# A decoder layer on one core: a new mixing order from engine queues, rotations in one scratch slot, gates that may move, and an output projection finished token tile by token tile

## The reference, cut to what matters

```python
h = rms_norm(x, ln_mix_pre);  p = h @ w_in                    # split into the branches' inputs and 3 * 1024 gate logits
y_a = dsa_attention(rotate(q), rotate(k), v, rotate(iq), rotate(ik), iw)   # index scores, top 128 keys of a query, softmax
y_b = rms_norm(gated_delta_rule(conv_silu(q, k, v), g, beta)) * silu(z)    # chunks, triangular inverse, scan
y_c = rms_norm(retention(rotate(q), rotate(k), v)) * silu(g)
merged = sum_i sigmoid(gate_i) * (y_i @ w_branch_i)
x = x + rms_norm(merged @ w_out, ln_mix_post)
x = x + rms_norm(square(relu(rms_norm(x, ln_mlp_pre) @ w_up)) @ w_down, ln_mlp_post)
```

## Time and profile before

| | |
|---|---|
| median of 3 runs | 2124.4 us (2123.76 to 2124.95) |
| the profiled execution | 2125.75 us, of which its span 2123.5 us |
| mean granted clock of TensorE | 0.961 of full |
| PE busy | 1977.4 us, 93% of the span |
| DVE, ACT, POOL busy | 47%, 21%, 53% |

### The profile page before, as it was taken

One profiled execution on the slowest core, in us unless ns is written; L12 is line 12 of the kernel. 1 busy time (PEld: TensorE's weight loads), 2 busy tenths in 40 slices (PEclk: granted clock), 3 DMA queues, 4 the chain that ended last, 5 costly groups with the idle time before them and its releaser, 6 DMA issues. The chain is left out here.

```text
span 2123.5 us, 25297 instructions
## 1 busy us (share of the span) xinstructions
PE 1977.4 (93%) x8942; PEld 1588.6 (75%) x8942; DVE 1004.9 (47%) x1616; ACT 450.9 (21%) x865; POOL 1130.0 (53%) x913
## 2 busy tenths in 40 slices
PE   7989978999998999999789899889999979999996
PEld 5856666778886888888668666667788868888885
DVE  4753666643434650361446436586334446404504
ACT  2152223321312100010112422242222131000101
POOL 4643331346665566666646424303567746666665
PEclk9999998999999999999889999899999989999998
DMA  6331220112322233222233212111224223223222
GB/s 251 100 110 58 57 81 24 57 60 99 139 97 82 80 99 99 96 92 99 96 133 99 95 60 72 60 40 50 70 96 143 90 69 100 98 92 98 99 98 79
DMA packets 73334, 192.07 MB, mean 90 GB/s; under 512 B 18528, under 2 KB 31008, under 8 KB 72224
## 3 DMA queue, kind: packets, MB, share of 16 engines
q1 hardware_dynamic: 46368, 173.22, 24.2%
q10 hardware_dynamic: 26880, 17.67, 2.8%
HBM read 179.81 MB, written 11.06 MB: 90 GB/s over the span
## 5 line engine op out<-in xcount | busy, mean ns | idle before, releaser
L803 POOL TENSOR_TENSOR w_lo<-raw,w_hi 128x1024 fp32r<-128x1024 f32 x296 | 726.5, 2455 | 24.7
L799 POOL TENSOR_TENSOR w_hi<-raw,tabs 128x1 fp32r<-128x1 f32 x296 | 65.5, 221 | 938.9 <-PE psD L838 724.5
L836 PE MATMUL psD<-a_hi,w_hi 128*128 128x512 f32 (+1 forms) x960 | 389.3, 406 | 15.5 <-DVE a_lo L1537 14.2
L837 PE MATMUL psD<-a_lo,w_hi 128*128 128x512 f32 (+1 forms) x960 | 378.5, 394 | 0.0
L838 PE MATMUL psD<-a_hi,w_lo 128*128 128x512 f32 (+1 forms) x960 | 378.4, 394 | 0.0
L800 POOL TENSOR_SCALAR w_hi<-raw 128x1023 fp32r<-128x1023 f32 x296 | 319.5, 1079 | 0.0
L836 PEld LDWEIGHTS psD<-a_hi,w_hi 128*128 128x128 f32 (+1 forms) x960 | 182.0, 190 | 60.1 <-DVE a_lo L1537 16.3
L837 PEld LDWEIGHTS psD<-a_lo,w_hi 128*128 128x128 f32 (+1 forms) x960 | 181.6, 189 | 41.4 <-issue 4.6
L838 PEld LDWEIGHTS psD<-a_hi,w_lo 128*128 128x128 f32 (+1 forms) x960 | 181.1, 189 | 41.9 <-issue 2.2
L836 PE MATMUL psM<-a_hi,w_hi 128*128 128x512 f32 x512 | 200.2, 391 | 0.3
L837 PE MATMUL psM<-a_lo,w_hi 128*128 128x512 f32 x512 | 199.3, 389 | 0.0
(11 more groups left out here) (238 smaller groups left out, 3091.4 us busy)
## 6 DMA issues: line engine op xcount, KB each, us to landing
raw<-in_ws SPq DMA_DIRECT2D x298, 512.0 KB, 3.3
out<-x SPq DMA_DIRECT2D x12, 512.0 KB, 2.6
tabs<-in_tab SPq DMA_DIRECT2D x2, 3072.0 KB, 12.9
x<-rows_d ACTq DMA_DIRECT2D x4, 1024.0 KB, 5.8
x<-out ACTq DMA_DIRECT2D x2, 2048.0 KB, 8.6
x<-in_x SPq DMA_DIRECT2D x4, 512.0 KB, 5.6
mt_d<-bw ACTq DMA_DIRECT2D x8, 256.0 KB, 2.3
x<-x_d ACTq DMA_DIRECT2D x8, 256.0 KB, 3.2
```

What stands on the lines that cost most here:

```text
L799: pool.tensor_tensor(w_hi[:, s, 0:1], raw[:, s, 0:1], T("ones")[:, 0:1], ALU.mult)
L803: pool.tensor_tensor(w_lo[:, s, :], raw[:, s, :], w_hi[:, s, :].bitcast(F32), ALU.subtract) \
L836: pe.matmul(out, lhi, rhi, start=start, stop=False)
L837: pe.matmul(out, lhi, rlo, start=False, stop=False)
```

## The change

The planner gets a clock for ACT, prices of four numbers (PE, ACT, DVE, and into how many pieces a step falls, so that engines overlap within it), widths for the attention steps, and 0.8 in place of 0.4 between steps of a stream. Scores with top-k and softmax with attention become two streams. The retention gates become a stream of their own, last in the list, which may run at any time (the last two only after the last rotation, whose scratch they overwrite). A rotation writes its cosine product straight to the destination and uses one scratch slot for the rest; the squares of `unit` and `fin` move to a new tile `sqs`.

Of the output projection two slabs stay in the stream. The other six are loaded by ACT's queue into memory that the branches have left, split by ACT and DVE in steps `stay` between the last merges, and stay there, so that PE can finish one token tile after the other (`out_tile`). The norm chain, the turning of x (`turn_x1`) and its split (`hi_x1`, `lo_x1`, 128 columns at a time) follow tile by tile; the first two slabs of the MLP run with 384 columns for tiles 0 to 2 and then with 128 columns for tile 3. The MLP's banks `psM` and `psD` change roles, `wide` is no longer zeroed (the first group copies into it), and the group loop is written out. In the diff the deepest indentation is reduced.

```diff
+STAYING = [("out", k, 2, half * S, S) for half, k in ((0, 4), (0, 6), (1, 0), (1, 2), (1, 4), (1, 6))]
+READY = ST - 1
...
-    slab = 2.6
-    cost = {"decay": (0, 1, .7), "prep": (2.7, 3.8, .7), "mt_out": (0, 0, .2), "blk_in": (0, 0, .2),
...
+    slab = 2.73
+    gate = (slab, .6, 0, 1)
+    cost = {"decay": (0, .6, 1.1, 1), "prep": (2.7, 1.2, 4.6, 2), "mt_out": (0, .1, 0, 1), "blk_in": (0, .1, 0, 1),
+            "solve": (0, 0, 7.5, 1), "y_out": (0, .2, 0, 1), "x_in": (0, .2, 0, 1), "lev": (0, 0, .9, 1),
+            "keys": (0, 0, 1.8, 1), "left": (.9, .6, 0, 1), "right": (1.8, 0, 1.8, 2), "scan_w": (.9, .6, 0, 1),
+            "scan_v": (1.8, .6, 0, 1), "scan_o": (2.7, .6, 1.6, 1), "ret": (4.3, .6, 2.4, 4), "turn": (0, 0, 1.6, 1),
+            "fin_sq": (0, .6, 0, 1), "fin": (.9, 1.2, 1.8, 1), "split": (0, .6, .9, 1), "half": (slab, 0, 0, 1),
+            "cv": (slab, .6, 0, 1), "rot": (slab, 1.2, .7, 1), "cg": (slab, .6, .7, 1), "z": (slab, .6, .7, 1),
+            "gate": gate, "mgate": gate, "mergeC": (slab, 0, 1.4, 1), "merge": (slab, 0, 3.2, 1)}
+    def takes(s):
+        w = s[1] + 1 if len(s) > 1 and s[0] in ("index", "top", "soft", "attend") else 0
+        if s[0] == "index":
+            return 1.75 * w, 8 * (.2 + .11 * w), 9 * (.13 + .17 * w), 8
+        if s[0] == "top":
+            return 0, 0, TOPK / TOPS / 4 * (.1 + .15 * w), 1
+        if s[0] == "soft":
+            return .86 * w, 4 * (.2 + .11 * w), 4 * (.6 + .32 * w), 4
+        if s[0] == "attend":
+            return 1.3 * w, .6 * w + .6, 0, w
+        return cost[s[0]]
...
-    attention = []
-    for tb in range(1, ST):
-        attention += [("index", tb)] + [("top", tb, part) for part in range(TOPS)]
-        for t in range(0 if tb == 1 else tb, tb + 1):
-            attention += [("soft", t), ("attend", t)]
-    attention += [("split", "C", h) for h in range(H)]
+    scores, softs = [], []
+    for tb in range(ST):
+        if tb:
+            scores += [("index", tb)] + [("top", tb, part) for part in range(TOPS)]
+        softs += [("soft", tb), ("attend", tb)]
+    softs += [("split", "C", h) for h in range(H)]
     dense = [("cv", i) for i in range(4)] + [("rot", r) for r in range(5, ROTS)] + [("cg", h) for h in range(H)]
-    dense += [("gate", "C", n) for n in range(KT)]
+    filler = [("gate", "C", n) for n in range(KT)]
...
-             ("soft", 0): [("turn", ROTS - 1)], ("gate", "C", 0): [("turn", ROTS - 1), ("fin", "C", 3)],
-             ("cg", 0): [("unit", 7)], ("split", "C", 0): [("fin", "C", 3)], ("mergeC", 0): [("split", "C", 3)],
+             ("soft", 0): [("turn", ROTS - 1)], ("gate", "C", 6): [("turn", ROTS - 1)],
+             ("cg", 0): [("unit", 7)], ("split", "C", 0): [("fin", "C", 3)], ("mergeC", 0): [("split", "C", 3), ("gate", "C", 7)],
              ("z", 0): [("split", "C", 3)], ("mgate", "A", 0): [("fin", "C", 3)],
              ("split", "A", 0): [("attend", ST - 1), ("mergeC", 3)]}
     for r in range(5, ROTS):
         after["turn", r] = [("rot", r)]
         after["rot", r] = [("turn", r - 2)]
-    shifts = 2.2
+    for tb in range(1, ST):
+        after["soft", tb] = [("top", tb, TOPS - 1)]
+        after["top", tb, TOPS - 1] = [("soft", tb - 1)]
...
-    dense = [s for d in dense for s in ([d] if d[0] == "split" else [("half", *d), d])]
+    dense, filler = ([s for d in what for s in ([d] if d[0] == "split" else [("half", *d), d])]
+                                     for what in (dense, filler))
     for s in list(after):
-        if s in dense:
+        if s in dense + filler:
             after["half", *s] = after.pop(s)
-    streams = [attention, rotations, chunks, even, odd + last, retention, dense]
+    streams = [scores, softs, rotations, chunks, even, odd + last, retention, dense, filler]
...
+    slabs = {len(streams) - 2, len(streams) - 1}
+    halved = None
     def ready(i):
+        if halved is not None and i in slabs and i != halved:
+            return 1e9
         return max([free[i]] + [ends.get(s, 1e9) for s in after.get(streams[i][0], ())])
...
+        if i in slabs:
+            halved = i if s[0] == "half" else None
+        t, c, d, k = takes(s)
+        begin = max(pe, at) if t else at
+        end = begin + t
         if t:
-            pe = max(pe, at) + t
+            pe = end
+        if c:
+            act = end = max(max(act, begin) + c, end + c / k + .2)
         if d:
-            dve = max(dve, at, pe + a if t or a else 0.0) + d
-        ends[s] = (dve if d else max(pe, at) + a) + (shifts if s[0] == "rot" else landing.get(s[0], 0))
-        free[i] = pe if streams[i] is dense else ends[s] + 0.4
+            dve = end = max(max(dve, begin) + d, end + d / k + .2)
+        ends[s] = end + landing.get(s[0], 0)
+        free[i] = pe if i in slabs else ends[s] + margin
...
-    o += [("split", "B", h) for h in range(H)] + merges("B", 0)
-    return o
+    tail = merges("B", 0)
+    for j in range(len(STAYING)):
+        tail.insert(5 + 2 * j, ("stay", j))
+    return o + [("split", "B", h) for h in range(H)] + tail
...
-    for half in range(2):
-        add(f"out{half}", *(("out", i, 2, half * S, S) for i in range(0, KT, 2)))
+    add("out0", *(("out", i, 2, 0, S) for i in range(0, STAYING[0][1], 2)))
...
+        with ExitStack() as o:
+            pg = sb("pg", [P, D], where=o)
+            s_hi = sb("s_hi", [P, len(STAYING), SLAB], F32R, where=o)
+            with ExitStack() as u:
+                s_raw = sb("s_raw", [P, len(STAYING), SLAB], where=u)
+            s_lo = sb("s_lo", [P, len(STAYING), SLAB], F32R, where=o)
...
+        def x1_T(t, k):
+            banks = (psM[0:2], psD[0:2], psM[0:2], psM[2:4])[t]
+            return banks[k // (KT // 2)][:, cut(k % (KT // 2))]
...
-        done(nslab([psM[t][:, :] for t in range(ST)], slab_in("out0", i), 2 * i, 2, S, i == 0, i == 3))
+        done(nslab([psM[t][:, :] for t in range(ST)], slab_in("out0", i), 2 * i, 2, S, i == 0, False))
     outs = [bank(DENSE["out1"] + t)[:, :] for t in range(ST)]
...
-    for i in range(3):
-        done(nslab(outs, slab_in("out1", i), 2 * i, 2, S, i == 0, False))
...
-    pe.wait_ge(sem("gained"), ST)
-    for t in range(ST - 1):
+    def out_tile(t):
+        for j, (_, k, ks, c, _) in enumerate(STAYING):
+            if t == 0:
+                pe.wait_ge(sem("s_lo"), j + 1)
+                pe.wait_ge(sem("a_lo"), KT + k + 2)
+            ins = nslab(outs if c else [psM[i][:, :] for i in range(ST)], j, k, ks, S,
+                        c > 0 and k == 0, k == KT - 2, ts=[t], w=(s_hi, s_lo))
+            if k == KT - 2:
+                ins.then_inc(sem("out_tile"), 1)
+    def turn_x1(t):
         pe.wait_ge(sem("diag_pre_mlp"), t + 1)
+        for i in range(2):
+            if t == 2:
+                pe.wait_ge(sem("a_lo"), 2 * KT + KT // 2 * (i + 1))
+            else:
+                pe.wait_ge(sem("gained"), (1, 2, None, 5)[t] + 2 * i)
+            for k in range(KT // 2 * i, KT // 2 * (i + 1)):
+                ins = pe.matmul(x1_T(t, k), x[:, t, cut(k)], wide[:, t, 0:P], start=True, stop=True)
+            ins.then_inc(sem("x1_turned"), 1)
+    for t in range(READY):
+        out_tile(t)
+    for t in range(READY - 1):
+        turn_x1(t)
+    out_tile(ST - 1)
+    turn_x1(READY - 1)
+    def up_tokens(i, t0, t1):
         for k in range(KT):
-            scaled_T(pe, (psM + psD)[k], t, k)
-    pe.wait_ge(sem("diag_pre_mlp"), ST)
-    for k in range(KT):
-        small_done(scaled_T(pe, (psM + psD)[k], ST - 1, k))
-    with pe.Fori(0, GROUPS) as g:
+            if i == 0:
+                pe.wait_ge(sem("a_lo"), 2 * KT + KT * (t1 - 1) + k + 1)
+            ins = tslab(psD[i][:, t0 * P:t1 * P], i % 2, ks=[k], cols=slice(t0 * P, t1 * P))
+        return ins
...
+            up_tokens(i, 0, READY)
+            if i == 1:
+                turn_x1(READY)
+                for j in range(2):
+                    done(up_tokens(j, READY, ST))
...
-            sig(act.copy(wt[to:to + n, r % 2, :], dbank(("rot", r))[at:at + n, :]),
+            sig(act.copy(wt[to:to + n, 6 + r % 2, :], dbank(("rot", r))[at:at + n, :]),
...
+    def stay(j):
+        if j == 0:
+            act.wait_ge(sem("stay_in"), 16 * len(STAYING))
+        sig(act.copy(s_hi[:, j, :], s_raw[:, j, :]), "s_hi")
...
+            act.wait_ge(sem("y_lo"), 3 * H)
+            for j in range(len(STAYING)):
+                act.dma_start(s_raw[:, j, :],
+                              wo[bass.ds(layer * len(STAYING) + j, 1)].rearrange("a p n -> (a p) n")) \
+                    .then_inc(sem("stay_in"), 16)
...
+    def hi_x1(t):
+        for k in range(KT):
+            act.wait_ge(sem("x1_turned"), 2 * t + k // (KT // 2) + 1)
+            sig(act.activation(a_hi[:, k, cut(t)], x1_T(t, k), ACT.Copy,
+                               scale=par_("gmlp")[:, k:k + 1]), "a_hi")
...
+        for half in range(2):
+            act.wait_ge(sem("out_tile"), 2 * t + half + 1)
```

(89 more changed lines are left out.)

147 lines of the change are left out of this document (48 added, 99 removed).

## The result

The changed kernel takes 2068.44 us (median of 4 runs, 2066.78 to 2071.23) where the kernel before takes 2124.08 beside it (4 runs, 2122.75 to 2124.95): a ratio of 0.9736, 95% interval 0.9724 to 0.9747. That is 55.6 us of the 64 forecast. Its profiled execution has a span of 2069.0 us.

A forecast was written before the change was run, and what follows sets the result against it. PE, busy 93%, bounds the kernel; only its idle stretches and half-clock slices can give time back. 2 x (27 mixing order + 5 passage) = 64 from 2125.75 gives 2061.8, as median 2060; range 2020 to 2100.

The forecast's parts named there:

- The mixing order: Mixing stage: slab halves and free gate slabs cover late chain steps; 27 us gained a layer, 54 in all.
- the four long waits: Planned part, second layer: PE's waits on DVE, 19.7 us together, all to be given back.
- I take 58 as it is: Planned part: PE's idle time and lost clock added, about 58 us a layer, their overlap left uncorrected.
- My mark for the planned part: Sign to check: planned part shortens from 346 to about 319 us; above 335 would be wrong.
- Separating scores from softmax adds nothing: Attention in the mixing stage: splitting the stream gains nothing, since 170 us of pure slabs follow its chain.
- The prices: Planner of the mixing order: new prices still leave out half clock and `psD` banks; no size given.
- `cv` will wait for four banks as before: Mixing stage: the plan leaves out the banks of `psD`, so this wait stays; no size given.
- Rotations in one slot, staying slabs: Mixing stage and output projection: both change nothing; the slabs cost 3 us a layer at worst.
- The passage: From output projection to MLP: norm and turning run tile by tile; 5 us gained a layer, bounds 1.6 to 7.
- the pieces: Passage: 48 matmuls of 384 and 48 of 128 columns replace 48 of 512; cost 2.5 to 7.9 us.
- POOL and DVE blocking each other: Rival, middle stretch: two-input DVE operations meet POOL more often, 8 us a layer, 2076; chance 0.12.
- The slower case: Rival, mixing order: misplaced filler halves delay ready chain steps, up to 2.7 us a miss, 2146; chance 0.09.

The follow-up runs named there:

- k2: Changed kernel with the eight retention gates put back into the dense stream behind the last rotation and the retention's end: 2099.89 us, ratio 0.9874.
- k3: Changed kernel with scores and softmax again one stream in the old order: 2076.24 us, ratio 0.9771.
- k10: k3 combined with k5 (one attention stream, rotation 4 ahead of turn 2): 2071.37 us, ratio 0.9739.
- k4: Changed kernel with the planner's old prices, two clocks instead of three and the old margin: 2089.71 us, ratio 0.9825.
- k5: Changed kernel with rotation 4 ahead of turn 2, using a scratch slot of its own: 2058.12 us, ratio 0.9672.
- k1: Changed kernel with the whole old mixing order; new passage, one-slot rotations and staying slabs kept, plus a small `memset` edit: 2118.89 us, ratio 0.9962.
- k11: The changed kernel itself, unaltered, measured once more: 2066.62 us, ratio 0.9727.
- k6: Changed kernel with the first of the eight free gates moved in front of the planned part, ahead of cv-0: 2068.17 us, ratio 0.9715.
- k7: Changed kernel with only the passage to the MLP reordered, the last tile turned right after the first up slab's three token tiles: 2061.72 us, ratio 0.9695.
- k9: k5 and k7 together (rotation 4 ahead of turn 2, reordered passage): 2053.48 us, ratio 0.9663.
- k8: Changed kernel with nine unread 512-column matmuls in the 2.56 us wait behind the last output tile: 2070.53 us, ratio 0.9727.
- k12: k9 with the nine unread matmuls of k8: 2051.99 us, ratio 0.9642.

## Why the prediction was right, step by step

**The mixing order: right in kind, 27 a layer forecast, 22.1 and 23.2 measured.** Two sizes in that term were off, to opposite sides. Of idle time I gave back the sum of the four long waits, 19.7; they went, but idle time fell by 13.7, since smaller waits took some of their place (2.1 and 2.0 in the list after). Of the clock I gave back 7, and 15.6 came back. "I take 58 as it is", idle and clock added, is what hid this: in the gain the two overlap by about 6 us. That one size was too large by 6 and the other too small by nearly 9, with an overlap between them that I had left out, is why the sum came near; this is luck, and the mechanism, late steps of DVE now covered by slabs, is not. My mark for the planned part, 346 to 319 with anything above 335 wrong, was badly chosen: it shows 340, with about three slabs, 16 us, moved into it, so it compares as 324. Its idle time is 19.0 where I had 14. The fillers did what was said. k2 shows it from the other side: held back, they cost 29 us.

**"Separating scores from softmax adds nothing": the step that failed.** I argued from where the attention chain ends, and 170 us of slabs do follow it. But the chain's order on DVE also sets when the last rotation is turned, and PE stands in place for that. It is worth some 4 a layer by the time of k3 and 7 by k10, inside the gain that I had put down to the fillers.

**The prices.** I had no term for them alone and called the plan's blind spots the reason for a cautious clock. k4 puts 19 us on prices, ScalarE's clock and the margin together; which of the three was not tried.

**"`cv` will wait for four banks as before": right.** 3.0 us in the same place, and k5 shows that it was worth 12 to 14 us in the two layers, with what the clock did behind it.

**Rotations in one slot, staying slabs: nothing, right.** k1 has both and gains no more than the passage. The six subtractions took 1.2 to 3.35 us each, more than the 0.68 doubled, and stayed hidden. The loads took 8.1 us to land, not 3.3, and nobody waited for them.

**The passage: 5 a layer forecast, 4.1 and 5.3 measured.** Of its terms, idle behind the last tile was 2.56 (2.9 forecast), the last tile's evacuation 0.73 (0.6), slow clock 10 x (0.33 - 0.173) = 1.6 (2; it is there in three of the four layers that were traced of this kernel, k11's included, and nothing in the fourth), the pieces 48 x (0.173 + 0.111 - 0.227) = 2.7 (2.5 to 7.9). A 128-column pass costs 0.111, the cheap end. I took 5 to be safe against the dear one. Unforeseen were the 1.20 at 1704.29: since both first slabs are finished together, POOL can start the third only at 1700.58. These are 8.8, so with 4.7 gained the kernel before lost about 13.5 there and not 15. The Trainium skill (TensorE: Matmul & The Clock Gate, Back-to-back issue gap) gave 81 ns where the trace has 111 for this data; the measurement decides.

**The rivals.** POOL and DVE blocking each other was priced at 8 us a layer, for 2076. The block is there, and it grew: without the staying slabs DVE is busy 4.3 and 6.6 us longer in the two mixing stages for the same work, and in k1, with the old order, it is not. Both engines pay for it, as the staying slabs show, whose subtraction takes 1.2 alone and 3.3 beside POOL:

```profile
1604.30 1.21 DVE L1886 TENSOR_TENSOR s_lo<-s_raw,s_hi 128x1024 fp32r<-128x1024 f32 x1
...
1606.58 1.23 DVE L1886 TENSOR_TENSOR s_lo<-s_raw,s_hi 128x1024 fp32r<-128x1024 f32 x1 [1.07 <-ACT s_hi L1494]
...
1612.02 3.25 DVE L1886 TENSOR_TENSOR s_lo<-s_raw,s_hi 128x1024 fp32r<-128x1024 f32 x1 [4.22 <-ACT s_hi L1494]
```

```profile
1600.91 2.91 POOL L835 TENSOR_TENSOR w_lo<-raw,w_hi 128x1024 fp32r<-128x1024 f32 x1
...
1606.67 3.38 POOL L835 TENSOR_TENSOR w_lo<-raw,w_hi 128x1024 fp32r<-128x1024 f32 x1
```

At 1606.67 DVE had come first, and POOL took 3.38 in place of 2.40. The Trainium skill (SBUF — State Buffer, Who interferes with whom) calls it an exclusive lock; by that rule the trace agrees. What it costs in all was not measured. In one place a stretched sine stood on the path, and by its excess, 2.86 - 0.69, had 2.2 of the 3.0 us that PE waited there; it did before the change too, and k5 took it off. The slower case did not come: no long wait on ACT stands behind a gate or a `stay`.

## What to carry to other kernels

A list scheduler needs something that may stand anywhere, and it needs prices read from a trace; here the first was worth 29 us and the second 19. When two chains share a queue, look at what stands behind the long one on that engine, not only at where the chain ends. A wait of 3 us on the busiest engine cost 3 to 7 a layer here, by the clock that happened to follow it, so find the one operation that made it late and let nothing urgent queue behind it, rather than put work in front of it that takes the same buffer.

## What the runs showed of the hardware

One program, one instruction list: its two layers took 581.45 and 590.00 us in one execution (k3), and two executions of the changed kernel differ by 2 to 4 us a layer. The clock behind a short wait is the reason that the traces show. Eleven of the traces have the wait of 2.56 us behind the last output tile, in both layers. In 15 of these 22 places half clock (1.2 GHz) followed within 1.6 us, in 7 full clock (2.4 GHz) went on: in both layers of k6 and k7, and in the second of k4, k5 and k11. k11 is the changed kernel, which has half clock in both places in its other trace. Where it was looked at (the changed kernel, k7 and k9, second layer) PE had streamed output tiles for 22.8 us and more without a gap before it. The same holds of the wait of 3.0 us in front of `cv`: 6.8 us of half clock in both layers of one trace of the changed kernel, in the other none and 3.4. What decides is open; no run here tells it. Where unread matmuls stood in place of the 2.56 us (k8, k12) no half clock followed directly in any of four layers, which 7 of 22 layers show without them, and in one of the four there was half clock some 14 us later. Whoever compares two kernels by one trace each must look at the clock behind every wait first: it is worth 1.6 us at the one place and up to 4 at the other.
